# Turning the probabilities one place later, with a fourth buffer

## The reference

```python
h = rms_norm(x, norm_g)
proj = jnp.einsum('bsd,de->bse', h, w_in) + b_in
...
y_a = indexer_sparse_attention(a_q, a_k, a_v, i_q, i_k, i_w)      # 8 heads of 64, keys chosen by an indexer (top 128)
y_b = chunked_relpos_attention(b_q, b_k, b_v, rel_bias)           # 8 heads of 64, relative bias
...
y_c = mlstm_chunkwise(c_q, c_k, c_v, c_i, c_f + f_bias, c_o)      # 4 heads of 128, matrix memory with decay
y_c = head_layer_norm(y_c, c_norm_w)
branches = jnp.stack([y_a * jax.nn.silu(a_z), y_b * jax.nn.silu(b_z), y_c * jax.nn.silu(c_z)], axis=2)
y = jnp.einsum('bsnw,nwd->bsnd', branches, w_branch)
merged = jnp.sum(jax.nn.sigmoid(gates) * y, axis=2)
return x + jnp.einsum('bsd,de->bse', merged, w_out)
```

## Time and profile before

| | |
|---|---|
| median of 3 runs | 1298.9 us |
| the profiled execution's own time | 1299.06 us |
| its span, first to last instruction | 1297.3 us |
| mean granted TensorE clock | 0.996 of full |
| PE busy | 1267.9 us, 98% |
| PE weight loads | 1063.4 us, 82% |
| DVE busy | 698.8 us, 54% |
| ACT busy | 620.0 us, 48% |
| GpSimd busy | 604.1 us, 47% |
| items' stretch, layer 0 and layer 1 | about 110 to 420 and 745 to 1010 us |

### The profile page before, as it was taken

The page is one execution under the profiler, slowest core; times in us unless marked ns, Lnnn a source line. Parts: engine busy times, 40 slices in busy tenths (PEclk is TensorE's granted clock), DMA queues, the critical chain, the costliest instruction groups (busy, mean ns, idle before and its releaser), DMA issues.

```text
span 1297.3 us, 19654 instructions
## 1 busy us (share of the span) xinstructions
PE 1267.9 (98%) x6438; PEld 1063.4 (82%) x6438; DVE 698.8 (54%) x1440; ACT 620.0 (48%) x1137; POOL 604.1 (47%) x759
## 2 busy tenths in 40 slices
PE   8999999999999999999999999999999999999997
PEld 6788888888987888887888888888888878888875
DVE  6789797844445221123687888886544631121143
ACT  6445667675534332333255465677654433333332
POOL 6654333422235555455675633343222455555462
PEclk9999999999999999999999999999999999999998
DMA  7223211221322323323242221122112222332321
GB/s 292 82 89 106 66 50 57 73 82 50 107 73 60 109 83 97 105 89 112 93 163 89 90 94 54 50 65 90 57 50 109 80 81 84 102 100 86 105 98 65
DMA packets 37047, 116.35 MB, mean 90 GB/s; under 512 B 4080, under 2 KB 4464, under 8 KB 36720
## 3 DMA queue, kind: packets, MB, share of 16 engines
q1 hardware_dynamic: 34672, 111.24, 25.7%
q10 hardware_dynamic: 2304, 4.20, 1.1%
HBM read 111.23 MB, written 4.19 MB: 89 GB/s over the span
## 4 chain that ended last, share of the span: by engine, by line
PE 83%; DVE 9%; ACT 4%; issue 2%; POOL 1%; DMA 0%; ACTq 0%; SPq 0%; DVEq 0%; POOLq 0%
PE acc L640 68%; PE ps_o L767 5%; PE ps_t L754 3%; DVE score L1270 2%; PE ps_t L745 2%; PE ps_o L774 1%; PE ps_s L723 1%; DVE top L1269 1%; PE ps_s L729 1%; DVE att_c L1404 1%; DVE ak_s L1243 1%; ACT prob L1015 1%; PE spare L705 1%; PE spare L784 1%; ACT z_tanh L867 0%
## 5 line engine op out<-in xcount | busy, mean ns | idle before, releaser
L595 POOL TENSOR_TENSOR w_lo<-w_raw,w_hi 128x256 fp32r<-128x256 f32 x744 | 590.6, 824 | 672.8 <-ACT w_hi L832 672.7
L640 PE MATMUL acc<-h_hi,w_hi 128*128 128x512 f32 x1120 | 448.5, 400 | 0.7 <-POOL h_lo L606 0.7
L640 PE MATMUL acc<-h_lo,w_hi 128*128 128x512 f32 x1120 | 439.6, 393 | 0.0
L640 PE MATMUL acc<-h_hi,w_lo 128*128 128x512 f32 x1120 | 292.9, 395 | 0.0
L832 ACT ACTIVATE w_hi<-w_raw 128x1024 fp32r<-128x1024 f32 (+1 forms) x210 | 201.8, 961 | 121.0 <-PE acc L640 92.5
L640 PEld LDWEIGHTS acc<-h_hi,w_hi 128*128 128x128 f32 x1120 | 211.0, 188 | 41.3 <-POOL h_lo L606 1.8
L640 PEld LDWEIGHTS acc<-h_lo,w_hi 128*128 128x128 f32 x1120 | 211.0, 188 | 38.9
L640 PEld LDWEIGHTS acc<-h_hi,w_lo 128*128 128x128 f32 x1120 | 205.3, 188 | 39.8
L1417 DVE SCALAR_TENSOR_TENSOR gated<-prob,acc 128x512 f32<-128x512 f32 x16 | 11.0, 688 | 247.6 <-PE acc L640 247.6
L1067 ACT ACTIVATE prob<-acc,par_half 128x512 f32<-128x512 f32 x48 | 33.1, 690 | 148.1 <-PE acc L640 148.1
L1015 ACT ACTIVATE prob<-prob,neg_max 128x128 f32<-128x128 f32 (+3 forms) x128 | 70.7, 552 | 20.4 <-DVE neg_max L1305 19.9
(11 more groups left out here) (244 smaller groups left out, 1792.8 us busy)
## 6 DMA issues: line engine op xcount, KB each, us to landing
w_raw<-w_full SPq DMA_DIRECT2D x162, 512.0 KB, 3.4
w_raw<-w_mix SPq DMA_DIRECT2D x48, 256.0 KB, 2.6
rel<-rel ACTq DMA_DIRECT2D x16, 256.0 KB, 2.7
xT<-x SPq DMA_DIRECT2D x4, 512.0 KB, 6.2
stage<-x_tok SPq DMA_DIRECT2D x4, 512.0 KB, 9.9
xT<-x SPq DMA_DIRECT2D x1, 2048.0 KB, 9.3
x_kept<-xT SPq DMA_DIRECT2D x1, 2048.0 KB, 8.9
xT<-x_kept SPq DMA_DIRECT2D x1, 2048.0 KB, 8.1
```

The costliest lines, as they stand in the source:

```text
L595: last = pool.tensor_tensor(w_lo[:, slot, part, :], w_raw[:, raw, part, :], w_hi[:, slot, part, :].bitcast(F32), ALU.subtract)
L640: last = pe.matmul(acc[slot][:, :], w[:, slot, k, :], x[:, k, :], start=(i == 0), stop=(i == 3 * nk - 1))
```

## The change

There are four `prob` buffers (PROBS) for three. In A and B the turn stands three places behind its scores (`back` 4) where it stood two behind, and the values four behind where they stood three. The exp stays one place behind. The mLSTM keeps its distances, but its exp waits for the item four before. `flush` pushes four empty places. To make room for the buffer, `ones` shrinks from 512 to 128 columns, and the scan reads one column of it, broadcast.

```diff
-        mlstm = any(m is not None and m >= 64 for m in flying[-4:])
-        for back, kind in ((1, "exp"), (2, "turn_p"), (3, "values")) if mlstm else ((2, "exp"), (3, "turn_p"), (4, "values")):
+        mlstm = any(m is not None and m >= 64 for m in flying)
+        for back, kind in ((1, "exp"), (2, "turn_p"), (3, "values")) if mlstm else ((2, "exp"), (4, "turn_p"), (5, "values")):
...
     def flush():
-        for _ in range(3):
+        for _ in range(4):
...
-        ones = sb("ones", [P, SEQ])
+        ones = sb("ones", [P, P])
...
-        prob = sb("prob", [P, 3, SEQ])
+        prob = sb("prob", [P, PROBS, SEQ])
...
-                            if n < 67:
-                                act.wait_ge(turn_full, l * ITEMS + n - 2)
+                            if n < 64 + PROBS:
+                                act.wait_ge(turn_full, l * ITEMS + n - PROBS + 1)
                             else:
-                                act.wait_ge(turn_free[(n - 3) % 2], l * (ITEMS // 2) + (n - 3) // 2 + 1 + FREE)
+                                act.wait_ge(turn_free[(n - PROBS) % 2], l * (ITEMS // 2) + (n - PROBS) // 2 + 1 + FREE)
...
-                        link(dve.tensor_tensor_scan(decay[:, SUM_AT[s]:SUM_AT[s] + w], ones[0:CH, 0:w], f_row[:, s * P:SEQ], 0.0,
+                        link(dve.tensor_tensor_scan(decay[:, SUM_AT[s]:SUM_AT[s] + w], ones[0:CH, 0:1].broadcast_to([CH, w]), f_row[:, s * P:SEQ], 0.0,
                                                     ALU.mult, ALU.add))
```

More of the change, by code:

```diff
@@ L32 @@
 IDX_HEADS = 4
+PROBS = 4
 TOPK = 128
@@ L753, in _ @@
                             for s in range(t + 1):
-                                last = pe.transpose(ps_t[n % 2][:, s * P:(s + 1) * P], prob[:, n % 3, s * P:(s + 1) * P], ident)
+                                last = pe.transpose(ps_t[n % 2][:, s * P:(s + 1) * P], prob[:, n % PROBS, s * P:(s + 1) * P], ident)
                             last.then_inc(turn_full, 1)
@@ L1014, in _ @@
                             act.wait_ge(max_ready, l * 64 + n + 1)
-                            act.activation(prob[:, n % 3, 0:(t + 1) * P], prob[:, n % 3, 0:(t + 1) * P], ACT.Exp,
+                            act.activation(prob[:, n % PROBS, 0:(t + 1) * P], prob[:, n % PROBS, 0:(t + 1) * P], ACT.Exp,
                                            bias=neg_max[:, n % 4:n % 4 + 1], scale=-1.0,
@@ L1027, in _ @@
                             for s in range(t + 1):
-                                last = act.activation(prob[:, n % 3, s * P:(s + 1) * P], ps_s[use % 2][:, s * P:(s + 1) * P],
+                                last = act.activation(prob[:, n % PROBS, s * P:(s + 1) * P], ps_s[use % 2][:, s * P:(s + 1) * P],
                                                       ACT.Exp, bias=source_t[:, s, h:h + 1])
@@ L1303, in _ @@
                                 mask = key_mask[:, MASK_AT[t]:MASK_AT[t] + w] if t else consts[:, K_CHUNK:K_CHUNK + P]
-                            dve.tensor_tensor_reduce(out=prob[:, n % 3, 0:w], in0=ps_s[use % 2][:, 0:w], in1=mask, scale=-1.0,
+                            dve.tensor_tensor_reduce(out=prob[:, n % PROBS, 0:w], in0=ps_s[use % 2][:, 0:w], in1=mask, scale=-1.0,
                                                      scalar=3.0e38, op0=ALU.add, op1=ALU.min,
@@ L1314, in _ @@
                             w = (t + 1) * P
-                            dve.scalar_tensor_tensor(prob_t[:, n % 2, 0:w], ps_t[n % 2][:, 0:w], 0.25 * P ** -0.5, prob[:, n % 3, 0:w],
+                            dve.scalar_tensor_tensor(prob_t[:, n % 2, 0:w], ps_t[n % 2][:, 0:w], 0.25 * P ** -0.5, prob[:, n % PROBS, 0:w],
                                                      ALU.mult, ALU.mult).then_inc(turn_free[n % 2], 1)
```

## The result

The changed kernel takes 1305.3 us in the median of 6 runs (1303.75 to 1306.92). The kernel before, run beside it, takes 1298.6 (6 runs, 1298.2 to 1299.1). The ratio is 1.0051, 95% interval 1.0040 to 1.0061: 6.7 us slower. I had forecast 1301.2 and a range up to 1304.6; both are missed, on the slow side.

What follows compares the result with a forecast made beforehand. TensorE, busy 98% of the span, was taken as the bound. Layer 0 at +1.0 us and layer 1 at +1.3 gave +2.3 on the profiled 1299.1; from the 1298.9 median, 1301.2 us, range 1296.0 to 1304.6.

Steps and rivals of the forecast that it cites:

- the exchange of waits: On PE, turns stop waiting for the exponential (7.1 us); values wait for ACT's copy instead, above 7 us in sum.
- place 56: Where item 56's scores are issued: PE's idle time was to shrink by 0.1 us in both layers.
- which layer 0 lacks: The wait at 932.45 us, seen in layer 1 only: 0.3 us more idle, counted for layer 1 alone.
- first rival: ACT not late as read, copy ready when PE arrives: all 7.1 us of waits go, 1291.8 us; chance 0.17.
- place 35: Where item 35's scores are issued: values wait for a copy behind the late exponential, start 219.97; idle grows 0.3 us.
- the places: At places 24 and 44 of both layers, values start about 0.1 us after DVE's division, PE idle 1.2 to 1.6 us.
- scan: The scan reading one broadcast column costs 0; far ends +2.1 or -1.1 us per layer.
- the start: Layer start: a turn's 0.5 us wait goes, but PE then meets item 1's maximum, leaving 0.4 us gained.
- New idle 1.34 for 0.82: Handover at place 24: PE reaches it 0.82 us earlier, DVE's pair ends 179.86, values at 179.96; +0.5 us.
- the stop absorbs what PE had gained or lost earlier in the layer: Place 44: DVE's gapless stretch doesn't wait for PE, so its 1.56 us stop swallows earlier shifts; 1.2 us later per layer.
- It may come again, or not, or at another place. I keep it: The granted-clock drop after the wait at 284.80 in layer 0, costing 1.6 us, was kept in the forecast.
- slower rival: The new stop at place 44 also drops the clock, 1.6 us in each layer: +5.5, 1304.4 us; clock or slow scan 0.14.

Runs made afterwards that it cites:

- e3: Changed kernel with ACT's copy of the turned block put ahead of the exponential; 1306.0 us, ratio 1.0059 to the kernel before.
- e1: Changed kernel with the old distances, leaving the fourth buffer, short ones, broadcast scan column and mLSTM wait; 1299.3 us, ratio 1.0000.
- e13: Changed kernel with only the last four top-k rounds of query tile 3 moved to places 9, 12, 15 and 17; 1299.2 us.
- e14: Changed kernel with only the gate rows from the 384-column scan on moved one projection unit later; 1304.3 us.
- e9: Changed kernel with both DVE moves: four top-k rounds to places 9, 12, 15, 17 and gate rows one unit later; 1298.7 us.
- e10: Kernel before with both DVE moves: four top-k rounds to places 9, 12, 15, 17 and gate rows one unit later; 1296.2 us.
- the light DVE: Four top-k rounds and one 384-column subtraction left out of the changed kernel, 1298.0 us, and of the kernel before, 1296.0 us.
- e11: Changed kernel with top-k rounds and gate rows moved to other places on DVE, plus ACT's copy ahead of the exponential; 1291.05 us.
- e15: Kernel before, old distances, with top-k rounds and gate rows moved on DVE and ACT's copy ahead of the exponential; 1304.5 us.
- e2: Kernel before with the values alone put one place later, turn and three buffers unchanged; 1306.8 us, ratio 1.0076.

## Why the prediction was wrong

**Right: the exchange of waits.** Forecast: the turn stops waiting, the values wait in its place, over 7 us in sum. Measured: 7.1 us gone, 7.7 come. The sum is in part luck, for two of its members were wrong. At place 56 I had 0.1 us less and found 1.1 less in each layer: ahead of the exponential ACT had waited 3.6 us for DVE's gated in before; in the changed kernel it waits 2.5 us there, for PE's projection. Its exponential comes 0.7 us later than in before, PE 1.9, and so PE finds the copy done. At place 59 I had nothing in layer 0, "which layer 0 lacks", and both layers stop 1.46 us: layer 0 lacked the wait in before only because the clock drop had made PE late. The first rival (all waits go, 1291.8) failed for the reason given, ACT's order; e3 shows it from the other side, since with the copy ahead 4.3 of the 7.7 us went. At place 35 the values start 219.69, 0.3 before the forecast 219.97, and the place changed the lateness by 0.0 for +0.3.

**Right: the places.** Four handover stops, at 24 and 44 of both layers, each ending 0.10 or 0.11 us after the division. Right too: scan, buffers and ones at nothing (e1), the start at -0.4 a layer (-0.3), PE's busy time.

**Wrong in size: "New idle 1.34 for 0.82" at place 24.** The idle is 179.53 - (177.06 + 0.33) = 2.14 us. I had PE ready for the values at 178.62, the old time less the old stop. It was ready at 177.39. The difference of 1.23 us is the start (0.3) and the one place of work that the change puts off: a turn of 384 and its values, 0.92 us, no longer stand ahead of this point. They are owed later, so they are not won, and they bring PE to the stop sooner. DVE was done 0.44 earlier than I had it. Net +1.3 (layer 0) and +1.0 (layer 1) for +0.5. The same work was left out at place 44: PE's ready time there, 246.04, still has the turn of 256 columns and the values of 128 in front of it, 0.37 us, that the change puts off.

**Wrong: "the stop absorbs what PE had gained or lost earlier in the layer".** I forecast 1.2 us of lateness from the layer's start to place 45 in all, with place 24 inside it. Measured is -0.3 + 1.3 + 1.0 = 2.0 in layer 0 and 1.8 in layer 1 without its clock drop: place 24's share stayed and place 44 came on top. I had read that DVE doesn't wait for PE from 222 on the earlier trace rows, and took that for not depending on PE at all. But DVE comes to that stretch behind waits for PE, in before already:

```profile
215.19 0.56 DVE L1305 CUSTOM_DVE_ANT_0 prob<-ps_s,rel 128x384 f32<-128x384 f32 x1 [1.28 <-PE ps_s L729]
```

So what PE loses or gains at place 24 moves DVE's list as a whole, and the stop at 44 stays as it is. The runs show it both ways: layer 1's clock drop behind place 24 put DVE's list 1.6 us back and left the stop at 1.07, and e13 came 2.2 us sooner and stopped 1.08. Absorbed is only what PE gains behind that last wait: in e3 1.5 us at place 35, of which 1.3 went again at 44. In layer 0 it looks as if DVE's list had not moved, since what PE was late at place 34 (1.0) and the work put off there (a turn of 512 and its values, 1.25) nearly cancel: the maximum of place 34 starts at 214.98 for 215.19, that of place 36, where the stretch begins, at 222.54 for 222.76.

Even so att_b ended at 247.98, not at 247.50. Two of DVE's operations in the stretch took longer than in before, 1.02 for 0.69 us and 0.91 for 0.55:

```profile
226.54 1.02 DVE L1257 TENSOR_TENSOR bq_s<-bq,bq_s 64x512 fp32r<-64x512 f32 x1
...
235.88 0.91 DVE L1282 TENSOR_SCALAR turn<-pad,par 128x512 f32<-128x512 f32 x1
```

Less the 0.22 by which the list began sooner this is 0.47, all of the difference. Why they took longer isn't shown. These 0.5 us and the 0.37 of work put off make up the 0.8 by which the forecast missed layer 0 up to place 45. With 0.6 in layer 1 this is the largest error of the sum.

**Wrong: "It may come again, or not, or at another place. I keep it".** The profiled pair has one drop each, before at 286, after at 816 behind the stop at place 24 of layer 1. But to keep 1.6 us on both sides was wrong: before's drop had hidden a wait and cost 0.4 net, the changed kernel's cost 1.6, so 1.2 us of the 4.65 come from here. The stretch of the changed kernel (us, PE busy and count, granted clock, DMA share, GB/s):

```profile
816.00:821.00 5.00, 4.62 (x16) 0.66 0.00 0
```

PE had stood 1.98 us before it. But the median run of the changed kernel is 1.6 us above its profiled one, the runs at a mean clock of 0.992 take 1306.4 and 1306.9, those at 0.995 and 0.996 take 1303.75 to 1305.35. The slower rival (a stop of this kind costs the clock, 1304.4) came nearest, and had 0.14 for its chance; it named place 44, and e13 and e14 put more of it on place 24.

**The sum.** Forecast +2.3 on the profiled run, measured +4.65. Of the 2.35 between them, 1.4 come from the two steps on the handover, 0.6 from the first product (7.96 for 7.81) and from behind place 63, 0.4 from place 53 (+0.1 for -0.1 a layer). From place 56 on the errors cancel to -0.2, which is luck: -1.0 a layer at place 56 against +1.2 for the wait that before's drop had hidden and +0.2 to +0.3 a layer from smaller ones. Of the other 2 us that bring the medians to 6.7 apart, 1.6 go with the lower mean clock of the changed kernel's other executions.

**Open.** Which stop draws a clock drop in a given run is not settled: the stop at 24 of layer 1 drew one in the changed kernel's profile and none in e14's, with the same wait of 2.0 us. Open too is why the longer distance costs 2.5 us in the medians when the stops are gone in both kernels (e9 and e10), and 2.0 with the light DVE.

## What to carry to other kernels

An item turned or multiplied one place later shifts its waits to the next consumer, unless the engines that work in list order are told to serve the older item first; and that swap pays only once the older item's input is old (e11 against e15). Before putting a handover of a shared accumulator one place later, read what the freeing engine has in its list between the two places, and count the work that the consumer no longer has ahead of it. An engine with no gap for 20 us is the bound there though its busy share is 54%: move its divisible work into its own idle gaps first, and measure the change again. Such a stretch takes back what is gained inside it, but it moves with whatever its engine waited for ahead of it: look at the last wait before the gapless stretch begins.

## What the runs showed that I had not expected

- A broadcast column as a scan's operand costs the same as a full row: 0.94 us for 384 columns in both kernels.
- The mean granted clock of a run goes with much of the scatter: 0.001 of it goes with 1.1 us between e9's runs at 0.992 and 0.995 (1299.9 and 1296.6) and with 1.2 between e2's ends. e11 spans 0.8 us, e2 with clocks from 0.989 to 0.997 spans 9.8 (1304.86 to 1314.68). Fewer stops don't always mean a narrower band: e9 spreads over 4.5 us, e13 with one stop more a layer over 1.7. Medians of two versions can so differ by more, or less, than their traces: the stop at 44 is worth 2.6 us between the traces of e13 and e9 and 0.5 between their medians.
- Apart from the program's two ends, the clock fell to its lower level of 1.2 GHz (0.50) for 2 to 4 us at a time in these profiles, each time at or behind an idle stretch of PE of about 1 us or more; but most waits of that length were followed by none.
- A clock drop can cost less than its 1.6 us, when it makes PE late for a wait that then isn't there (net 0.4 in the kernel before).
